# Up projections of 256 tokens: high and low token halves beside each other in one 512-column matmul

## The reference

```python
def squared_relu_mlp(h, w_up, w_down):
    return jnp.square(jax.nn.relu(h @ w_up)) @ w_down
...
def swiglu(h, w_gate_up, w_down):
    g, u = jnp.split(h @ w_gate_up, 2, axis=-1)
    return (jax.nn.silu(g) * u) @ w_down
```

## Time and profile before

| | |
|---|---|
| median of 3 runs | 1911.78 us (1906.54 to 1918.8) |
| profiled execution | 1916.42 us, span of its instructions 1914.6 us |
| mean granted TensorE clock | 0.942 |
| PE busy | 1761.6 us, 92% |
| DVE busy | 1072.7 us, 56% |
| ACT busy | 704.2 us, 37% |
| HBM traffic | 309.18 MB, 161 GB/s over the span |

### The profile page before, as it was taken

The page is one execution under the profiler, slowest core; times in us unless marked ns, Lnnn a source line. Parts: engine busy times, 40 slices in busy tenths (PEclk is TensorE's granted clock), DMA queues, the critical chain, the costliest instruction groups (busy, mean ns, idle before and its releaser), DMA issues.

```text
span 1914.6 us, 25663 instructions
## 1 busy us (share of the span) xinstructions
PE 1761.6 (92%) x10636; PEld 1411.5 (74%) x10636; DVE 1072.7 (56%) x1634; ACT 704.2 (37%) x878; POOL 84.5 (4%) x87
## 2 busy tenths in 40 slices
PE   4999998899999998999889997987999979779998
PEld 1786456777777777764579995675999766669996
DVE  3664456554444445764566775555666464656654
ACT  2323345321313123433444444363433243633332
POOL 1020000100000001100000001000000010010000
PEclk9999887999999999998989998988999979889999
DMA  9325870224344334258545555431555553335542
GB/s 341 115 104 187 314 271 1 96 86 149 133 149 150 139 132 145 86 182 305 201 152 197 198 181 184 165 132 63 179 177 168 197 202 118 131 110 176 176 168 96
DMA packets 172371, 309.18 MB, mean 161 GB/s; under 512 B 3264, under 2 KB 54720, under 8 KB 171616
## 3 DMA queue, kind: packets, MB, share of 16 engines
q1 hardware_dynamic: 168592, 293.98, 43.8%
q10 hardware_dynamic: 3376, 12.00, 1.8%
q0 software_dynamic: 288, 1.57, 0.2%
HBM read 305.44 MB, written 2.10 MB: 161 GB/s over the span
## 4 chain that ended last, share of the span: by engine, by line
PE 77%; DVE 12%; ACT 4%; DMA 3%; issue 2%; POOL 1%; DVEq 0%; ACTq 0%; POOLq 0%; SPq 0%
PE bank L576 59%; PE twin L576 15%; DVE ring_r L1223 3%; PE bank L585 2%; ACT arena_r L1985 2%; DMA ring<-in_w_in 2%; DMA ring<-in_w_mod 2%; ACT arena L1985 2%; DVE arena L1223 1%; POOL rs L2396 1%; DVE params L1223 1%; DVE arena L1315 1%; DVE arena_r L1223 0%; DVE X L1733 0%; DVE actT_r L1318 0%
## 5 line engine op out<-in xcount | busy, mean ns | idle before, releaser
L576 PE MATMUL bank<-arena_r 128*128 128x512 f32 (+2 forms) x2128 | 702.0, 376 | 14.7 <-DVE arena_r L1855 6.7
L1223 DVE TENSOR_TENSOR ring_r<-ring,arena_r 128x4096 fp32r<-128x4096 f32 (+4 forms) x98 | 394.3, 4023 | 203.6 <-ACT arena_r L1985 202.8
L576 PEld LDWEIGHTS bank<-arena_r 128*128 128x128 f32 x2128 | 405.7, 191 | 94.7 <-issue 8.1
L1985 ACT ACTIVATE arena_r<-ring 128x4096 fp32r<-128x4096 f32 (+4 forms) x96 | 323.5, 3370 | 386.8 <-PE bank L576 129.8
L576 PE MATMUL twin<-actT_r,arena_r 128*128 128x256 f32 x1408 | 254.7, 284 | 1.1 <-DVE actT_r L1223 1.1
L576 PE MATMUL bank<-ring_r,arena_r 128*128 128x512 f32 x624 | 246.1, 394 | 0.0
L576 PE MATMUL bank<-arena_r,actT_r 128*128 128x512 f32 (+3 forms) x624 | 222.0, 387 | 11.9 <-DVE ring_r L1223 5.0
L1985 ACT ACTIVATE arena<-bank 128x512 f32<-128x512 f32 (+6 forms) x195 | 91.8, 471 | 360.8 <-PE bank L576 276.5
L576 PEld LDWEIGHTS twin<-actT_r,arena_r 128*128 128x128 f32 x1408 | 220.1, 192 | 1.7 <-DVE actT_r L1223 1.7
L576 PE MATMUL twin<-actT_r,ring_r 128*128 128x256 f32 x704 | 199.4, 283 | 0.0
L576 PE MATMUL bank<-ring_r,actT_r 128*128 128x512 f32 (+3 forms) x496 | 184.6, 372 | 0.0
(11 more groups left out here) (193 smaller groups left out, 1679.8 us busy)
## 6 DMA issues: line engine op xcount, KB each, us to landing
ring<-in_w_mod SPq DMA_DIRECT2D x24, 2048.0 KB, 9.2
ring<-in_w_ada SPq DMA_DIRECT2D x24, 2048.0 KB, 9.0
ring<-in_w_gate_up SPq DMA_DIRECT2D x44, 1024.0 KB, 7.7
ring<-in_w_down SPq DMA_DIRECT2D x20, 2048.0 KB, 7.9
ring<-in_w_up SPq DMA_DIRECT2D x16, 2048.0 KB, 7.8
ring<-in_w_in SPq DMA_DIRECT2D x12, 2048.0 KB, 11.0
ring<-in_w_out SPq DMA_DIRECT2D x8, 2048.0 KB, 11.2
ring<-in_w_down SPq DMA_DIRECT2D x8, 1792.0 KB, 7.6
```

What stands on the lines that cost most here:

```text
L576: ins = nc.tensor.matmul(out_, lhsT, rhs, start=start, stop=stop)
L1223: return v.tensor_tensor(o, x, y, op)
L1985: return nc.scalar.activation(o, x, func, **kw)
```

## The change

In layer 1 of the first trunk and in the second trunk, the low half of the tokens lies in columns 256 to 511 behind the high half. `beside` does each contraction tile in two matmuls instead of three: the weights' high part against all 512 columns, and their low part against the high half, which is added in the upper 256 columns of the bank. One bank thus holds two sums of 256 columns, and they are added outside PE: ACT copies the upper half into SBUF (`minor_ready`), DVE adds the lower half of the bank to it.

In layer 1 ACT copies for all four tiles of a chunk, DVE adds for all four; for odd m ACT then takes relu out of SBUF when DVE has added, and goes on as before. The square of even tiles becomes one fused instruction (max with 0, times itself), so these have as many DVE instructions as before. In the second trunk gate and value lie in a bank each, of rings "s" and "a"; ACT copies both upper halves, waits for DVE's add of the gate and takes tanh; DVE adds the gate, adds the value, and forms the product from SBUF. The scratch is in `hid_lo`'s unused token tiles and in `params`. In layer 1 the low half moves from the arena to the columns behind the high one.

The list of semaphores gains `minor_ready`; the rest of the diff:

```diff
--- before.py
+++ after.py
@@ -349,6 +349,8 @@
         hid2_lo, hid2_lo_r = carve(5632, 22, S), carve(5632, 22, S, buf=arena_r)
         sg2 = params[:, 2048:2560].rearrange("p (a n) -> p a n", a=2)
         junk2 = params[:, 2560:3072]
+        gate2 = junk2.rearrange("p (a n) -> p a n", a=2)
+        value2 = params[:, 3072:3584].rearrange("p (a n) -> p a n", a=2)
 
 
         bank = [ctx.enter_context(nc.psum_tensor(f"bank{i}", [P, 512], f32)) for i in range(5)]
...
@@ -618,6 +620,17 @@
                         pe.wait_ge(who, nth(who))
                         k["turned"] -= 1
                     three(out_, lhs(i), rhs(i), i == order[0], i == order[-1], inc if i == order[-1] else None)
+
+            def beside(out_, lhs, inc):
+
+                for i in range(KT):
+                    x, last = lhs(i), i == KT - 1
+                    if k["turned"]:
+                        who = actp_ready if i % 2 else act_ready
+                        pe.wait_ge(who, nth(who))
+                        k["turned"] -= 1
+                    mm(out_[:, :], x[0], actT_r[:, i, :], i == 0, False)
+                    mm(out_[:, S:2 * S], x[1], actT_r[:, i, 0:S], False, last, inc if last else None)
 
             def contract(out_, lhs, rhs, inc, n=KT):
 
@@ -948,8 +961,12 @@
                         w = weights(("up1", l, c))
                         for m in range(4):
                             b, filled = take("va"[m % 2])
-                            linear(b[:, 0:n], lambda i: [x[:, i, m * P:(m + 1) * P] for x in w],
-                                   lambda i: [x[:, i, 0:n] for x in (actT_r, act_lo_r)], filled)
+                            if l == L - 1:
+                                beside(b, lambda i: [x[:, i, m * P:(m + 1) * P] for x in w], filled)
+                            else:
+                                linear(b[:, 0:n], lambda i: [x[:, i, m * P:(m + 1) * P] for x in w],
+                                       lambda i: [x[:, i, 0:n] for x in (actT_r, act_lo_r)], filled)
+                            mark["up1", l, c, m] = k["va"[m % 2]]
                             if m % 2 == 1 and gates:
                                 gate(l, 5, *gates.pop(0))
                     if l == 0:
@@ -1161,11 +1178,10 @@
                 for c in range(F2 // 256):
                     w = weights(("up2", l, c))
                     for m in range(2):
-                        b, filled = take("s")
-                        for g in range(2):
-                            linear(b[:, S * g:S * (g + 1)],
-                                   lambda i: [x[:, i, S * g + m * P:S * g + (m + 1) * P] for x in w],
-                                   lambda i: [x[:, i, 0:S] for x in (actT_r, act2_lo_r)], filled if g == 1 else None)
+                        for g, r in enumerate("sa"):
+                            b, filled = take(r)
+                            beside(b, lambda i: [x[:, i, S * g + m * P:S * g + (m + 1) * P] for x in w], filled)
+                        mark["up2", l, 2 * c + m] = k["s"], k["a"]
                 for half in range(2):
                     banks = [take("v") for t in range(TS)]
                     mark["y", l, 2 + half] = k["v"]
@@ -1635,7 +1651,10 @@
                 for half in range(2):
                     split(after(("out1", l, half)))
                     residual1(tiles1(l), half, gates, (lambda t: norm_tile(t, 2 * l + 1)) if half else None)
-                turned(tiles1(l), act_lo, act_lo_r)
+                if l == L - 1:
+                    turned(tiles1(l), act2_lo, act2_lo_r)
+                else:
+                    turned(tiles1(l), act_lo, act_lo_r)
                 dve.wait_ge(ga_in, nth(ga_in, 32))
                 gates = gates_of(l)
                 tiles = slice(0, len(tiles1(l)))
@@ -1648,7 +1667,25 @@
                             low, high = hid_lo[:, tiles, i, :], hid_hi[:, tiles, i, :]
                             if l == 0 and m == 1:
                                 split(after(("up1", l, c)))
-                            if m % 2 == 0:
+                            if l == L - 1:
+                                at = mark["up1", l, c, m]
+                                both = hid_lo[:, 2:4, i, :]
+                                if m % 2 == 0:
+                                    b = filled()
+                                else:
+                                    dve.wait_ge(a_filled, at)
+                                    b = AB[(at - 1) % 2]
+                                dve.wait_ge(minor_ready, nth(minor_ready))
+                                ins = tt(both, b[:, 0:S].rearrange("p (t n) -> p t n", n=P), both, ALU.add)
+                                if m % 2 == 0:
+                                    step(ins, v_emptied)
+                                    step(v.scalar_tensor_tensor(out=low, in0=both, scalar=0.0, in1=both,
+                                                                op0=ALU.max, op1=ALU.mult))
+                                    step(v.tensor_copy(high, low))
+                                else:
+                                    ins.then_inc(a_emptied, 1)
+                                    dve.wait_ge(hsq_ready, nth(hsq_ready))
+                            elif m % 2 == 0:
                                 b = filled()
                                 step(v.tensor_scalar(low, b[:, 0:n].rearrange("p (t n) -> p t n", n=P), 0.0, None,
                                                      ALU.max), v_emptied)
@@ -1927,12 +1964,19 @@
                 for m in range(F2 // P):
                     if m % 2 == 0:
                         split(after(("up2", l, m // 2)))
+                    g, gate_, value = sg2[:, m % 2, :], gate2[:, m % 2, :], value2[:, m % 2, :]
+                    b = filled("s")
+                    dve.wait_ge(minor_ready, nth(minor_ready))
+                    step(tt(gate_, b[:, 0:S], gate_, ALU.add), s_emptied)
+                    n = mark["up2", l, m][1]
+                    dve.wait_ge(a_filled, n)
+                    dve.wait_ge(minor_ready, nth(minor_ready))
+                    tt(value, AB[(n - 1) % 2][:, 0:S], value, ALU.add).then_inc(a_emptied, 1)
+                    dve.wait_ge(a_emptied, n)
                     dve.wait_ge(sg_ready, nth(sg_ready))
-                    b = filled("s")
-                    g = sg2[:, m % 2, :]
-                    step(v.scalar_tensor_tensor(out=g, in0=g, scalar=1.0, in1=b[:, 0:S], op0=ALU.add, op1=ALU.mult))
-                    step(v.scalar_tensor_tensor(out=hid2_lo[:, m, :], in0=g, scalar=0.5, in1=b[:, S:512],
-                                                op0=ALU.mult, op1=ALU.mult), s_emptied)
+                    step(v.scalar_tensor_tensor(out=g, in0=g, scalar=1.0, in1=gate_, op0=ALU.add, op1=ALU.mult))
+                    step(v.scalar_tensor_tensor(out=hid2_lo[:, m, :], in0=g, scalar=0.5, in1=value,
+                                                op0=ALU.mult, op1=ALU.mult))
                     step(v.tensor_copy(hid2_hi[:, m, :], hid2_lo[:, m, :]))
                     rest(hid2_lo[:, m, :], hid2_lo_r[:, m, :], hid2_hi[:, m, :], hid_ready)
                     if m == 1 and l < L - 1:
@@ -2024,7 +2068,7 @@
                 if n:
                     squared(tiles, n)
                 act.wait_ge(modT_ready, nth(modT_ready))
-                lo = act_lo if n < 2 * L else act2_lo
+                lo = act_lo if n < 2 * L - 1 else act2_lo
                 n = P * len(tiles)
                 for ft in range(1, KT, 2):
                     b = filled()
@@ -2245,11 +2289,23 @@
                 for q in range(4):
                     for c in (2 * q, 2 * q + 1):
                         split(after(("up1", l, c)))
-                        for m in (1, 3):
+                        for m in range(4):
                             i = 4 * (c % 2) + m
-                            b = filled()
-                            low = hid_lo[:, tiles, i, :]
-                            step(f(low, b[:, 0:n].rearrange("p (t n) -> p t n", n=P), ACT.Relu), a_emptied)
+                            low, both = hid_lo[:, tiles, i, :], hid_lo[:, 2:4, i, :]
+                            if l == L - 1:
+                                at = mark["up1", l, c, m]
+                                act.wait_ge(a_filled if m % 2 else v_filled, at)
+                                b = (AB if m % 2 else VB)[(at - 1) % 2]
+                                step(f(both, b[:, S:2 * S].rearrange("p (t n) -> p t n", n=P), ACT.Copy), minor_ready)
+                            if m % 2 == 0:
+                                continue
+                            if l == L - 1:
+                                nth(a_filled)
+                                act.wait_ge(a_emptied, nth(a_emptied))
+                                step(f(low, both, ACT.Relu))
+                            else:
+                                b = filled()
```

(13 more changed lines are left out.)

## The result

The kernel after the change takes 1946.65 us (median of 6 runs, 1943.56 to 1949.68), the one before 1911.99 in its 6 runs: a ratio of 1.0184 [1.0168, 1.0201]. It is slower by 34.7 us; the forecast was 1943. The profiled execution has a span of 1945.2 us against 1914.6.

What follows compares the result with a forecast made beforehand. PE was taken to set the end on the whole. Profiled 1916.4 us + 28.0 (layer one's waits) + 0 (second block) + 3.4 (clock) = 1947.8; with the median 4.6 below the profiled execution, 1943, range 1918 to 1962.

Steps and rivals of the forecast that it cites:

- the first rival: Whole kernel: ACT and DVE keep up using their free time, only PE's gain is left, 1899 us; chance 0.13.
- The layout of a round: Layer one's MLP: instruction order of PE, ACT and DVE lengthens a round from 44.82 to 51.85 us, +28 over four rounds.
- 2.2 for two terms: Layer one's second down chunk: PE waits 1.5 us for its split and 0.7 more for the bank DVE empties after it.
- My tile waits of 3.4 us: Layer one's first down chunk: PE waits for hidden tiles 5, 6 and 7, 3.4 us in all.
- my four waits: PE's waits in a layer-one round: first down split 2.2, hidden tiles 3.4, second down split 1.5, bank 0.7 us.
- The clock: Layer one's rounds: waits lower PE's clock, half of 1.7 us lost per round, +3.4 us; ends 0 and 13.6.
- The second rival: Second block's seven waits per layer and layer one's rounds keep the clock down, 34 us more, 1977 us; chance 0.09.
- PE's gain: Second block and layer one: 960 triples of matmuls become pairs, 0.360 to 0.347 us each, 12.8 us of PE time.
- The second trunk: Its up chunks: an ACT and DVE loop of 11.82 us against PE's 11.10; 0 us per layer, bounds -1.8 and +1.8.
- The fifth up2 chunk of 12.1 us: Second block: slack lasts four chunks of 11.10 us, the fifth takes 12.1 and each later one 11.82.
- the 8.70 us: Second block: time from the first split's start until the split and the bank emptied by the gate add are ready for PE.

## Why the prediction was right

**Direction and place.** Layer one was to lose 28.0 us from waits on the two engines' order and 3.4 from the clock; the trace has +30.6 there, and the kernel with the change in layer one alone has the loss (ratio 1.0164 of 1.0184, within the intervals). The idle time of DVE and ACT, on which the first rival rested, was of no use; the kernel with more work on DVE and less order between the engines had no loss.

**The layout of a round.** From PE's start at 1030.60 (ACT's 1031.00 less 0.40), ACT's down split began at 16.26 (forecast 16.2), DVE's ended at 24.41 (24.33), the second down split began at 32.10 (32.0). PE waited 2.32 (2.2) and 2.13 (2.2 for two terms). This is arithmetic on an order of instructions, and it held to some 0.1 us. My tile waits of 3.4 us show as only 0.98: in their place PE went at a clock of 0.66 through these tiles. In round three idle (5.37) and PE's longer busy time (46.85 less the 44.38 of a round without waits, 2.47) are together 7.8, the sum of my four waits.

**The clock.** I took +3.4 us for it, with 0 and 13.6 as ends: half of one low stretch's loss in every round. The sum of it came out, the working did not. Rounds two and three of the kernel after have the same waits (2.32, 0.98 and 2.13 us; 2.32, 0.96 and 2.09). The clock fell behind the first wait in both, but behind the last in rounds two and four alone. Windows of the second down chunk of rounds two, three and four:

```profile
1071.73:1084.46 12.73, 12.73 (x49) 10.37 (x50) 7.77 (x6) 3.62 (x1) 0.00 (x0) 0.87 0.48 166
1125.59:1136.68 11.09, 11.09 (x49) 9.20 (x50) 7.76 (x6) 3.63 (x1) 0.00 (x0) 1.00 0.54 191
1177.79:1190.60 12.81, 12.80 (x48) 10.04 (x48) 3.35 (x5) 4.16 (x3) 0.00 (x0) 0.87 0.42 134
```

12.73 - 11.09 is the 1.6 us by which round two is longer than round three; twice that is 3.3 us for the clock. The low clock behind the first wait shows no cost: in the kernel with DVE's wait away PE waits 2.33 us there in rounds two and four, and the clock behind it was 0.66 in round two (1053.0 to 1058.0) and 1.00 in round four (1157.5 to 1162.5), yet PE began the second down chunk 16.15 and 16.16 us after that wait. The slower matmuls took time in which PE else waited for hidden tiles (1.32 us of waits in round two, 2.35 in round four). So 3.4 for 3.3 is in part luck: a whole loss in two rounds, not a half in each. What is left for the layout is 30.6 - 3.3 = 27.3 us against 28.0: round one is 5.3 us longer than before, round three 7.4, where I had 7.0 for each. The second rival, with 34 us more, is refuted: it was to decide by waits of 0.7 us lowering the clock, and those of 0.28 to 0.84 at the up2 chunks of the second trunk's layer 0 left it at 1.00.

**PE's gain.** The term was mis-sized: 6.3 us, not 12.8. I built a pair out of two cadences that were each measured in long rows of one size, and said that no row alternates them. Yet the earlier trace rows has the first 512 behind the last 256, at 1003.59, and the trace of the kernel before has the step behind it:

```profile
1003.83 0.40 PE L576 MATMUL bank<-ring_r,arena_r 128*128 128x512 f32 x1
```

That is 0.24 us, as in the kernel without copies and adds, where it comes in every pair. The error hardly mattered, since the change leaves PE's gain unused in both stages; that followed from the layout, and the kernel with three narrow matmuls shows it. The rule of the Trainium skill ("TensorE: Matmul & The Clock Gate", Back-to-back issue gap), which the page gives for isolated matmuls, would have given back an estimated 2.4 us for the 960 matmuls; the runs show 6.3 us with sizes alternating and, from the grouped cadence, 960 x 0.011 = 10.6 us. The measurement lies above the rule in either order.

**The second trunk.** I entered 0 with +1.8 per layer as the upper end; the traces have +1.8 and +1.7. ACT's splits are 11.91 us apart, where I had 11.82. Of the 0.09, 0.07 are the two tanhs of a loop, which read SBUF (next view). Ten loops make 0.9 of the 1.8, PE's last chunk at 11.31 instead of 11.10 makes 0.2. One interval per layer is 12.19 instead of 11.91: in layer 0 a tanh begins 0.38 us after the add that it waits for there, where others begin 0.10 after. That is 0.3 more; the remaining 0.4 I can't assign.

Groups by form of the kernel after (count, busy us, mean ns, idle before):

```profile
L1239 DVE TENSOR_TENSOR params<-twin,params 128x256 f32<-128x256 f32 x44 | 18.7, 424 | 1.5
L2029 ACT ACTIVATE params<-params 128x256 f32<-128x256 f32 x44 | 18.4, 418 | 118.0 <-DVE params L1239 117.8
L2029 ACT ACTIVATE params<-twin 128x256 f32<-128x256 f32 x44 | 17.0, 385 | 1.4
```

The add costs 0.42 as taken from the fused form in the earlier trace rows, and the copy 0.385. The tanh out of SBUF takes 0.418, not the 0.384 that it took out of PSUM.

**The sum.** Span against span the change costs 30.6 us, and my terms made 31.4: 28.0 for 27.3, 3.4 for 3.3, 0 for 3.5, and nothing for -3.5 in what both kernels do alike. That the last two cancel is luck. Median against median the change costs 34.7. The 4 us between these are that the profiled execution of before was 4.4 us above its median, that of after 0.5. By the medians 1943 was 3.65 us too low, a fifth of a per cent.

**Slips in the working.** "2 x 1408 + 704 of 2112" should be 1408 + 704 = 2112; the 704 triples are right. The fifth up2 chunk of 12.1 us doesn't follow from the 8.70 us: by these the fourth chunk would already be 11.36 and each later one 11.82, with the same sum of 126.7.

## What to carry to other kernels

Before work is moved from a bound engine to two with free time, write out their order over a stage: here free time was of no use where something that others need was queued behind a wait. A weight split or a copy for the next tile is worth putting ahead of waits for the other engine's result, and a chain ACT, DVE, ACT, DVE for one tile was better kept on one engine, though that engine then worked more. Matmuls of different sizes were a little cheaper in groups than in turn (0.004 us a pair).

## What the runs showed of the hardware

- The time from one matmul's start to the next depends on both sizes: 0.227 us in rows of 512 columns, 0.120 in rows of 256, but 0.24 and 0.115 in turn. A pair is 0.353 us in turn and 0.349 in groups of eight.
- The clock after a wait of PE can't be told from the wait's length alone. Behind 1.90 us it was 0.60, and behind 2.32 us 0.66 over the stretch at 1055. Behind 2.13 us in round two it fell (0.87 over the chunk), behind 2.09 in round three it stayed at 1.00. In the kernel with the copy ahead, waits of 0.62, 0.28, 0.64 and 1.77 us lie in a round with a clock of 1.00. What decides it stays open.
- Stretches in which all kernels have the same instructions differed by up to 7 us from trace to trace: the one between layer one's MLP and the first up2 (from split to split) took 186.4 us before, 183.0 in the kernel with the second trunk's change alone, 187.8 in that with layer one's and 189.6 in that with DVE's wait away. Differences of 3 us between kernels are better read stage by stage than from medians.
